# Router logits formed per token tile, an earlier first gather, and paired small matmuls in a transformer block with a mixture of experts

## The chip, the cores and the metric

The kernel is written for Trainium2, and it uses one NeuronCore of the chip. Its engines are TensorE (PE, matrix products), VectorE (DVE), ScalarE (ACT), GpSimd (POOL) and SyncE (SP, which here issues the large DMA transfers). They run side by side and wait for each other through semaphores. The metric is the device time of one execution in microseconds (us), lower is better. The time of the kernel before is the median of three runs.

## What is computed

One layer on 256 tokens of width 1024, all in float32: an attention branch in which each token reads its 64 best-scored tokens, a gated linear-attention branch (GLA) that works in chunks of 64 tokens, and then a mixture of 32 experts of which each token takes 4.

```python
h = _rmsnorm(x, norm1_g) * (1.0 + sc1) + sh1
proj = h @ w_in
...
# GLA, for one chunk of 64 tokens (step); S is the running state
qe = qn * jnp.exp(gn)
A = jnp.einsum('bhid,bhjd->bhij', qe, kn * jnp.exp(-gn))
A = jnp.where(causal, A, 0.0)
o = jnp.einsum('bhij,bhjv->bhiv', A, vn) + jnp.einsum('bhid,bhdv->bhiv', qe, S)
S = S * jnp.exp(g_last).swapaxes(-1, -2) + jnp.einsum('bhjd,bhjv->bhdv', kn * jnp.exp(g_last - gn), vn)
...
x = x + gt1 * (merged @ w_out)
h2 = _rmsnorm(x, norm2_g) * (1.0 + sc2) + sh2
x = x + gt2 * _moe(h2, router_w, router_b, w_gate_up, b_gate_up, w_down, b_down)
...
# _moe
logits = (xt @ router_w + router_b).astype(jnp.float32)
top_v, top_e = lax.top_k(logits, TOP_K)
wts = jax.nn.softmax(top_v, axis=-1)
...                      # each token to its 4 experts, gate and up products, SwiGLU, down product, weighted sum
```

## The kernel before

There are 256 tokens, so two token tiles of 128 (`t` = 0 and 1), and 1024 features, so eight feature tiles (`KT` = 8).

**First part.** TensorE goes through the weight pieces (512 columns each, 2 MB, four slots in turn) in the order written in `PIECES`. Each result goes to one of eight PSUM banks; the list `PLAN` numbers these tiles and says whether ACT ("A") or DVE ("V") takes each out. `begin` waits until the tile that held the bank eight places earlier is taken, and `full` tells the taker. The order of the engines' work is the order of the code: nothing is scheduled.

**Three small parts of GLA** lie in it. `AT` holds the 64x64 score blocks: 16 products, whose results for even chunks go to PSUM partitions 0 to 63 and for odd chunks to 64 to 127. `state_step(n)` makes the update of the state after chunk `n-1`: four products that contract over 64 rows, rows 0 to 63 of the array for odd `n` and 64 to 127 for even `n`. Tiles `o0` to `o3` are the outputs: 16 products with `AT` (64 rows, 64 columns) and 12 with the state (128 rows, 64 columns), written alternately.

**Router part.** After the last output piece (`wo3`), DVE adds the result to the residual (`take_wo`), ACT squares and sums it, `second_norm(t)` forms the inverse root and `h2`. TensorE transposes `h2` (tiles `hh0` to `hh3`; ACT copies them to `h2T`). Tile `rp` holds four partial sums of the logits for all 256 tokens, in four 32-row groups; ACT copies it, and four products with `stack` and the bias make the logits `rl`. DVE takes the four largest per token (`chosen`), TensorE counts with `before` (a strict triangle of ones) how many earlier tokens chose each expert (`rt`: ranks and totals). From this DVE forms `blocks` (blocks of 64 slots per expert), `slot_id` and, with the help of tile `te`, the tables that the expert loop reads (`tables_ready`).

**Expert loop.** It has one pass per block of 64 slots. A pass is made of gate and up products (32 products of 512 columns, in two column halves of the array, from `gu_slot`), the gather of the next block's tokens (`gather`, products of `h2` with the 0/1 matrix `sel`), its transposes into `xg`, and the down products (from `dn_slot`). The weights of expert 0 are loaded as soon as the slots are free of pieces; those of expert `e` >= 1 slot by slot as soon as the pass that used the slot last is done (SP, lines 343 and 348). So the loop's transfers start with the loop. The gather of block 0 stands ahead of the loop:

```python
            e0 = dve.value_load(table_e[0:1, 0:1], min_val=0, max_val=E - 1)
            select(e0)
            select_weights(e0, slice(0, 1))
```

Before its first product TensorE waits for `xg_out` (the gathered tokens), `selw_ready` and `selw_out`; the last is first signalled by DVE's `memset` of `selwT` (line 1001), which stands behind `select_weights` and thirteen tiny memsets.

Of the kernel before, what the change touches and what calls it, by code (L numbers as in the profile page):

```python
# [13 lines left out]
P = 128  # L14
# [21 lines left out]
    + [(f"vb{i}", "A") for i in range(4)] + [("s1a", "V"), ("s1b", "V"), ("va0", "A"), ("va1", "A")]  # L36
# [9 lines left out]
    + [(f"hh{i}", "A") for i in range(4)] + [("rp", "A"), ("rl", "V"), ("rt", "V"), ("te", "V"), ("wt", "A")]  # L46
# [21 lines left out]
def hybrid_block(nc, x, c, w_ada, b_ada, norm1_g, w_in, w_gate_lr, b_gate, gla_norm_g, w_branch_a, w_branch_b, w_out,  # L68
# [28 lines left out]
    with ExitStack() as ctx:  # L97
# [122 lines left out]
        eofw = sb("eofw", 177, [MAXB + 1, 3 * E])  # L220
        steps8 = small("steps8", [P, T // SLOTS])
# [164 lines left out]
        def _(pool):  # L386
# [34 lines left out]
            for i in range(3):  # L421
# [15 lines left out]
        def _(act):  # L437
# [174 lines left out]

            take("rp", (rpart[:], tile("rp")[:, 0:T], ACT.Copy, {}))
            act.wait_ge(rneg_ready, 1)
            for t in range(TT):
                step(A(eexp[:, t, :], lg[:, t, 0:E], ACT.Exp, bias=nr8[:, t:t + 1]), rexp_ready)

            take("wt", (wT[:], tile("wt")[0:E, 0:T], ACT.Copy, {}))


            act.wait_ge(gath_full, 1)
            step(A(gx[:], bank[2][:], ACT.Copy), gx_out)
            act.wait_ge(gxT_full, 1)
            step(A(xg[:].rearrange("p j s -> p (j s)"), bank[3][:], ACT.Copy), xg_out)
# [26 lines left out]
        def _(dve):  # L651
# [105 lines left out]
            def state(n):  # L757
                for half, name in enumerate((f"s{n}a", f"s{n}b")):
                    wait_tile(dve, name)
                    for j in range(2):  # L760
# [11 lines left out]
            state(1)  # L772
            state(2)
# [89 lines left out]
            def take_wo(i):  # L863
# [69 lines left out]
            wait_tile(dve, "rl")  # L933
            chain(V.tensor_copy(lg[:, :, 0:E], tile("rl")[:, 0:TT * E].rearrange("p (t e) -> p t e", e=E)), out_dve)
            for t in range(TT):
                chain(V.max(r8[:, t, :], lg[:, t, 0:E]))
                step(V.tensor_scalar(nr8[:, t:t + 1], r8[:, t, 0:1], -1.0, None, ALU.mult), rneg_ready if t == 1 else None)
# [12 lines left out]
            wait_tile(dve, "rt")  # L950
            counts = tile("rt")[:, TT * E:TT * E + E]
# [43 lines left out]
            select(e0)  # L995
# [56 lines left out]
        def _(pe):  # L1052
# [136 lines left out]
            for n in range(NCH):  # L1189
                r = 64 * (n % 2)  # L1190
                for h in range(GH):
# [8 lines left out]
            def state_step(n):  # L1200

                cn = n - 1
                r, t = 64 * (cn % 2), cn // 2
                for half, name in enumerate((f"s{n}a", f"s{n}b")):
                    ps = begin(name)
                    for j in range(2):
                        h = 2 * half + j
                        ins = M(ps[:, j * DV:(j + 1) * DV], kdt[r:r + 64, t, h * P:(h + 1) * P], vb[r:r + 64, t, h * DV:(h + 1) * DV],
                                start=True, stop=True)
                    full(ins)  # L1210
# [6 lines left out]
            state_step(3)  # L1217
# [56 lines left out]
            for i in range(4):  # L1274
                t, half = divmod(i, 2)
                ps = begin(f"o{i}")
                for n in (2 * t, 2 * t + 1):
                    r = 64 * (n % 2)
                    for j in range(2):
                        h = 2 * half + j  # L1280
# [32 lines left out]
            for i in range(4):  # L1313
                t, half = divmod(i, 2)
                pe.wait_ge(h2_ready, i + 1)
                transposes(f"hh{i}", h2, t, half)

            ps = begin("rp")
            wait_out(pe, "hh3")
# [153 lines left out]
```

## Time and profile before

| what | value |
|---|---|
| median of 3 runs | 1477.98 us (1476.35 to 1479.79) |
| the profiled execution's own time | 1480.57 us |
| its span, first to last instruction | 1478.2 us |
| mean granted TensorE clock | 0.984 |
| busy: PE, DVE, ACT, POOL | 1381.5, 498.0, 250.2, 10.6 us |
| HBM read | 482.00 MB, 327 GB/s over the span |
| passes of the expert loop | 36 |

The profile is of one execution, and times in it count from its first instruction. "Busy" is a sum over the whole span, so it doesn't say which engine sets the end at a given moment; the chain of waits does. The granted clock is a share of TensorE's full clock, and its two levels are 1.0 (2.4 GHz) and 0.5 (1.2 GHz). In the trace each float32 product shows as two MATMUL records, so x8 is four products.

### The profile page before, as it was taken

How to read it: one execution, taken by the hardware profiler on the slowest of the kernel's cores; microseconds unless marked ns; L12 is line 12 of the kernel's file. 1: busy time of each engine (PE TensorE's matmuls, PEld its weight loads, DVE VectorE, ACT ScalarE, POOL GpSimd, SP SyncE). 2: the span in 40 equal slices, each digit the busy share in tenths (PEclk: the TensorE clock that was granted, in tenths of full speed). 3: DMA queues.
4: the chain of work that ended last, by engine and by line, in shares of the span. 5: the costliest groups of instructions: out<-in, count | busy, mean ns of one | idle time of the engine just before them, and what ended most of it. 6: DMA issues, size and time to landing. Idle time of an engine off the chain costs nothing.

```text
span 1478.2 us, 17039 instructions
## 1 busy us (share of the span) xinstructions
PE 1381.5 (93%) x6263; PEld 618.4 (42%) x6264; DVE 498.0 (34%) x1029; ACT 250.2 (17%) x427; POOL 10.6 (1%) x34
## 2 busy tenths in 40 slices
PE   5999999999969999999999999999999999989996
PEld 3888445888533333333333333333333333223321
DVE  2150023555553323323323323323323323323233
ACT  2321014210021111111111111111111111111111
POOL 0000000100000000000000000000000000000000
PEclk8999999999969999999999999999999999999998
DMA  9643433699628449999699999979999999999994
GB/s 352 216 166 115 169 114 114 210 344 348 231 114 341 168 172 387 418 419 416 245 418 416 419 418 418 416 301 419 418 418 418 417 417 419 419 417 417 419 419 198
DMA packets 113087, 483.37 MB, mean 327 GB/s; under 512 B 10102, under 2 KB 10266, under 8 KB 80202
## 3 DMA queue, kind: packets, MB, share of 16 engines
q1 hardware_dynamic: 111666, 477.95, 81.2%
q0 software_dynamic: 1056, 4.06, 0.9%
q10 hardware_dynamic: 344, 1.07, 0.2%
q8 instruction: 14, 0.23, 0.1%
q14 instruction: 7, 0.06, 0.0%
HBM read 482.00 MB, written 1.05 MB: 327 GB/s over the span
## 4 chain that ended last, share of the span: by engine, by line
PE 72%; DMA 11%; SPq 9%; ACT 4%; issue 1%; DVE 1%; DVEq 0%; ACTq 0%
PE bank L1397 23%; PE bank L1091 14%; PE bank L1426 13%; DMA gu_slot<-in_w_gate_up 10%; PE bank L1100 7%; SPq L343 4%; SPq L348 4%; PE bank L1356 4%; PE bank L1372 3%; PE bank L1365 1%; DMA piece<-in_w_ada 1%; ACT gx L633 1%; ACT xg L635 1%; ACT actT L637 1%; PE bank L1404 1%
## 5 line engine op out<-in xcount | busy, mean ns | idle before, releaser
L1397 PE MATMUL bank<-gu_slot,xg 128*64 128x512 f32 x2304 | 517.1, 596 | 17.2 <-DMA gu_slot<-in_w_gate_up 16.5
L1397 PEld LDWEIGHTS bank<-gu_slot,xg 128*64 128x64 f32 x2304 | 158.5, 137 | 364.8 <-issue 307.5
L1426 PE MATMUL bank<-dn_slot,actT 128*64 128x512 f32 x1152 | 255.1, 595 | 24.7 <-ACT actT L637 24.7
L1011 DVE TENSOR_TENSOR rowt<-bank,gt 128x512 f32<-128x512 f32 x144 | 92.7, 686 | 389.7 <-PE bank L1372 388.4
L1091 PE MATMUL bank<-hT,piece 128*128 128x256 f32 x704 | 155.1, 382 | 0.0
L1426 PEld LDWEIGHTS bank<-dn_slot,actT 128*64 128x64 f32 x1152 | 79.3, 137 | 177.4 <-issue 144.2
L1091 PEld LDWEIGHTS bank<-hT,piece 128*128 128x128 f32 x704 | 134.6, 192 | 19.5 <-issue 1.1
L631 ACT ACTIVATE sig<-gcl 128x512 f32<-128x512 f32 x36 | 22.7, 630 | 567.7 <-DVE gcl L1029 567.7
L1029 DVE TENSOR_SCALAR gcl<-bank 128x512 f32<-128x512 f32 x36 | 24.9, 692 | 273.6 <-PE bank L1397 273.6
L1015 DVE TENSOR_TENSOR xs<-xs,rowt 128x512 f32<-128x512 f32 x144 | 93.1, 688 | 2.5
L1100 PE MATMUL bank<-piece,hT 128*128 128x512 f32 x192 | 83.4, 593 | 0.0
L1356 PE MATMUL bank<-h,sel 128*64 128x512 f32 x296 | 71.3, 603 | 3.0 <-DVE sel L983 3.0
L1372 PE MATMUL bank<-ysb,selwT 64*128 64x512 f32 x288 | 71.5, 615 | 0.0
L641 ACT ACTIVATE ysb<-bank 128x512 f32<-128x512 f32 x36 | 21.5, 598 | 248.9 <-PE bank L1426 248.9
L1100 PEld LDWEIGHTS bank<-piece,hT 128*128 128x128 f32 x192 | 36.2, 190 | 44.3 <-issue 44.2
L631 ACT ACT_TABLE_LOAD x36 | 46.2, 1283 | 1.2 <-issue 0.6
L890 DVE SCALAR_TENSOR_TENSOR modq<-piece,csig,modq 128x512 f32<-128x512 f32 x56 | 42.1, 752 | 2.0
L1356 PEld LDWEIGHTS bank<-h,sel 128*64 128x64 f32 x296 | 21.5, 139 | 45.7 <-issue 45.7
L1372 PEld LDWEIGHTS bank<-ysb,selwT 64*128 64x128 f32 x288 | 24.8, 186 | 31.8 <-issue 31.8
L1365 PE MATMUL bank<-ident,gx 128*128 128x128 f32 x148 | 24.3, 286 | 12.5 <-ACT gx L633 11.9
L1100 PE MATMUL bank<-piece,mergedT 128*128 128x512 f32 x64 | 27.9, 594 | 0.7 <-DVE mergedT L860 0.7
L1091 PE MATMUL bank<-ybT,piece 128*128 128x256 f32 x128 | 28.0, 379 | 0.0
(279 smaller groups left out, 787.1 us busy)
## 6 DMA issues: line engine op xcount, KB each, us to landing
gu_slot<-in_w_gate_up SPq DMA_DIRECT2D x256, 1024.0 KB, 17.4
dn_slot<-in_w_down SPq DMA_DIRECT2D x128, 1024.0 KB, 17.6
piece<-in_w_in SPq DMA_DIRECT2D x17, 2048.0 KB, 8.3
piece<-in_w_ada SPq DMA_DIRECT2D x12, 2048.0 KB, 12.9
piece<-in_w_branch_a SPq DMA_DIRECT2D x2, 2048.0 KB, 8.6
piece<-in_w_branch_b SPq DMA_DIRECT2D x2, 2048.0 KB, 8.7
piece<-in_w_out SPq DMA_DIRECT2D x2, 2048.0 KB, 8.5
xs<-in_x ACTq DMA_DIRECT2D x1, 1024.0 KB, 8.9
```

What stands on the lines that cost most here:

```text
L343: sp.dma_start(gu_slot[j][:], w_gate_up[0, e, j * P:(j + 1) * P, :] if isinstance(e, int) else w_gate_up[0, ds(e, 1), j * P:(j + 1) * P, : ...
L348: sp.dma_start(dn_slot[i][:], w_down[0, e, rows, :].rearrange("(i p) n -> p i n", p=P) if isinstance(e, int) else w_down[0, ds(e, 1), rows ...
L631: A(sig[:], gcl[:], ACT.Sigmoid, scale=ALPHA).then_inc(sig_ready, 1)
L890: chain(V.scalar_tensor_tensor(dst[:], w[:, k, :], csig[:, k:k + 1], dst[:], ALU.mult, ALU.add), modq_ready if k == KT - 1 else None)
L1011: ins = V.tensor_tensor(rowt[:, t, :], sum_bank[t][q][:], gt2[:, cols_], ALU.mult)
L1015: ins = V.tensor_tensor(xs[:, t, cols_], xs[:, t, cols_], rowt[:, t, :], ALU.add)
L1091: ins = M(ps[:, f * T:(f + 1) * T], w[:, k, a:a + P], src[:, k, :], start=(k == 0), stop=(k == KT - 1))
L1100: ins = M(ps[:], src[:, k, t * P:(t + 1) * P], w[:, k, :], start=(k == 0), stop=(k == KT - 1))
L1356: ins = M(bank[2][64 * q:64 * q + 64, :], sel[:, t, :], h2[:, t, 512 * q:512 * q + 512], start=(t == 0), stop=(t == TT - 1))
L1372: ins = M(sum_bank[t][q][:], selwT[64 * q:64 * q + 64, t * P:(t + 1) * P], ysb[64 * q:64 * q + 64, :], start=True, stop=True)
L1397: ins = M(bank[u][64 * q:64 * q + 64, :], xg[:, k % 4, 64 * (k // 4):64 * (k // 4) + 64], gu_slot[k][:, cols_], start=(k == 0), stop=(k == ...
L1426: ins = M(bank[5][64 * q:64 * q + 64, :], actT[:, f % 4, 64 * (f // 4):64 * (f // 4) + 64], dn_slot[f // 2][:, f % 2, 512 * q:512 * q + 51 ...
```

## The change

1. `state_step(1)` and `state_step(2)` are issued together, product by product in turn (rows 0 to 63 and rows 64 to 127 of the array), and DVE takes them in that order.
2. The products of `AT` and of `o0` to `o3` are reordered so that two that use different halves of the array stand next to each other.
3. `h2` is multiplied by `sc2g` in `take_wo`, before the inverse root is known; `second_norm` then needs one operation per half in place of two.
4. `rp`, its copy and the products with `stack` are gone. The logits of tile `t` are eight products of `h2T` (128x128, stationary) with the router weights (32 columns), and one with the bias; `rl0` stands between the transposes of `t` = 0 and those of `t` = 1.
5. Block 0 is always expert 0's (`steps8[:, 0]` is -1, so each expert has at least one block, even with no token), so its slots are the ranks themselves: `first_slot` and `sel` are made straight after `rt`, ahead of `blocks` and the tables, and the first gather stands ahead of tile `te`, into `bank[6]`, with its transposes in `bank[7]`, ahead of `wt`.

```diff
-    + [(f"hh{i}", "A") for i in range(4)] + [("rp", "A"), ("rl", "V"), ("rt", "V"), ("te", "V"), ("wt", "A")]
+    + [("hh0", "A"), ("hh1", "A"), ("rl0", "V"), ("hh2", "A"), ("hh3", "A"), ("rl1", "V"), ("rt", "V"), ("te", "V"), ("wt", "A")]
...
+            step.settle()
+            step(nc.gpsimd.memset(steps8[:, 0:1], -1.0))
...
                 chain(V.tensor_tensor(xv, xv, tmp[:], ALU.add), x2_ready)
+                cols_ = slice(512 * cc, 512 * cc + 512)
+                step(V.tensor_tensor(h2[:, t, cols_], xv, sc2g[:, cols_], ALU.mult))
...
-                    chain(V.scalar_tensor_tensor(h2[:, t, cols_], xs[:, t, cols_], rs[:, t:t + 1], sc2g[:, cols_],
-                                                 ALU.mult, ALU.mult))
-                    step(V.tensor_tensor(h2[:, t, cols_], h2[:, t, cols_], sh2[:, cols_], ALU.add), h2_ready)
+                    step(V.scalar_tensor_tensor(h2[:, t, cols_], h2[:, t, cols_], rs[:, t:t + 1], sh2[:, cols_],
+                                                ALU.mult, ALU.add), h2_ready)
...
             wait_tile(dve, "rt")
+            for t in range(TT):
+                step(V.scalar_tensor_tensor(first_slot[:, t:t + 1], tile("rt")[:, t * E:t * E + 1], 1.0, chosen[:, t, 0:1],
+                                            ALU.add, ALU.mult))
+            step.settle()
+            for t in range(TT):
+                ins = V.tensor_scalar(sel[:, t, :], iota[:], 1.0, first_slot[:, t:t + 1], ALU.add, ALU.is_equal)
+            ins.then_inc(sel_ready, 1)
...
-            select(e0)
             select_weights(e0, slice(0, 1))
...
             wait_out(pe, "vb3")
-            state_step(1)
+            for half in range(2):
+                begin(f"s1{'ab'[half]}")
+                begin(f"s2{'ab'[half]}")
+                for lower, upper in zip(state_half(1, half), state_half(2, half)):
+                    pass
+                full(lower)
+                full(upper)
             by_token("va", 0, hT)
-            state_step(2)
             by_token("va", 1, hT)
...
-                for n in (2 * t, 2 * t + 1):
-                    r = 64 * (n % 2)
-                    for j in range(2):
-                        h = 2 * half + j
-                        o_ = ps[r:r + 64, j * DV:(j + 1) * DV]
+                for j in range(2):
+                    h = 2 * half + j
+                    vcols = slice(h * DV, (h + 1) * DV)
+                    for n in (2 * t, 2 * t + 1):
+                        r = 64 * (n % 2)
                         a = (h * 2 + n // 2) * CHUNK
-                        ins = M(o_, AT[r:r + 64, a:a + CHUNK], vb[r:r + 64, t, h * DV:(h + 1) * DV], start=True, stop=(n == 0))
+                        ins = M(ps[r:r + 64, j * DV:(j + 1) * DV], AT[r:r + 64, a:a + CHUNK], vb[r:r + 64, t, vcols],
+                                start=True, stop=(n == 0))
+                    for n in (2 * t, 2 * t + 1):
+                        r = 64 * (n % 2)
                         if n > 0:
-                            ins = M(o_, qe[:, h, n * CHUNK:(n + 1) * CHUNK], S[n][:, h * DV:(h + 1) * DV], start=False, stop=True)
+                            ins = M(ps[r:r + 64, j * DV:(j + 1) * DV], qe[:, h, n * CHUNK:(n + 1) * CHUNK], S[n][:, vcols],
+                                    start=False, stop=True)
...
-            for r in range(2):
-                for q in range(4):
-                    k = 4 * r + q
-                    ins = M(ps[32 * q:32 * q + 32, 0:T], wr[:, k, :], h2T[:, k, :], start=(r == 0), stop=(r == 1))
...
+            for t in range(TT):
+                for half in range(2):
+                    pe.wait_ge(h2_ready, 2 * t + half + 1)
+                    transposes(f"hh{2 * t + half}", h2, t, half)
+                ps = begin(f"rl{t}")
+                for k in range(KT):
+                    if k % 4 == 0:
+                        wait_out(pe, f"hh{2 * t + k // 4}")
+                    M(ps[:, 0:E], h2T[:, k, t * P:(t + 1) * P], wr[:, k, :], start=(k == 0), stop=False)
+                full(M(ps[:, 0:E], ones[0:1, :], rb[:], start=False, stop=True))
...
+            pe.wait_ge(sel_ready, 1)
+            gather(bank[6])
+            ps = begin("te")
+            pe.wait_ge(eofc_ready, 1)
+            full(M(ps[0:3 * E, 0:MAXB + 1], eofw[:], ident[0:MAXB + 1, 0:MAXB + 1], start=True, stop=True))
+            pe.wait_ge(gx_out, 1)
+            gather_transposes(bank[7])
+            ps = begin("wt")
```

How the instructions stand on TensorE, at three places. The numbers with L are lines of each kernel's own file, and a name like `S_74` is the buffer `S2`.

First place: the outputs of GLA on TensorE (`AT` score blocks, `vb` values, `S_73` to `S_75` the states after chunks 0, 1 and 2). Of before, from the start of `o0`:

```order
L1283 MATMUL bank<-vb,AT 64x256 x3
L1285 MATMUL bank<-S_73,qe 64x256
L1283 MATMUL bank<-vb,AT 64x256
L1285 MATMUL bank<-S_73,qe 64x256
L1283 MATMUL bank<-vb,AT 64x256 x3
L1285 MATMUL bank<-S_73,qe 64x256
```

Of the kernel changed, the end of `o1` (token tile 0) and the start of `o2` (token tile 1):

```order
L1299 MATMUL bank<-vb,AT 64x256 x2
L1304 MATMUL bank<-S_73,qe 64x256
L1299 MATMUL bank<-vb,AT 64x256 x2
L1304 MATMUL bank<-S_74,qe 64x256
L1304 MATMUL bank<-S_75,qe 64x256
L1299 MATMUL bank<-vb,AT 64x256 x2
```

Before, each `AT` product but a few has a state product behind it; now two `AT` products stand together, and in token tile 1 two state products too.

Second place: the logits on TensorE, behind the last output piece (`h_85` is `h2`, `rpart` the copy of `rp`, `rb` the bias). Before:

```order
L1107 MATMUL bank<-ident,h_85 128x128 x16
L1324 MATMUL bank<-h2T,wr 32x256 x8
L1329 MATMUL bank<-stack,rpart 128x32
L1330 MATMUL bank<-rb,ones 128x32
L1329 MATMUL bank<-stack,rpart 128x32
L1330 MATMUL bank<-rb,ones 128x32
```

Changed:

```order
L1116 MATMUL bank<-ident,h_85 128x128 x8
L1342 MATMUL bank<-wr,h2T 128x32 x8
L1343 MATMUL bank<-rb,ones 128x32
L1116 MATMUL bank<-ident,h_85 128x128 x8
L1342 MATMUL bank<-wr,h2T 128x32 x8
L1343 MATMUL bank<-rb,ones 128x32
```

The logits of token tile 0 now stand ahead of the transposes of token tile 1.

Third place: on TensorE from the end of `rt` (last product of the counts) to the expert loop (`eofw` is the input of `te`, `wts` that of `wt`, `sel` and `gx` those of the gather and of its transposes). Before:

```order
L1339 MATMUL bank<-chosen,ones 128x32
L1342 MATMUL bank<-ident,eofw 96x49
L1348 MATMUL bank<-ident,wts 32x128 x2
L1378 TENSOR_LOAD table_n
L1378 ISA x2
L1356 MATMUL bank<-h_85,sel 64x512 x4
L1365 MATMUL bank<-ident,gx 128x128 x4
```

Changed:

```order
L1352 MATMUL bank<-chosen,ones 128x32
L1358 MATMUL bank<-h_85,sel 64x512 x4
L1374 MATMUL bank<-ident,eofw 96x49
L1367 MATMUL bank<-ident,gx 128x128 x4
L1382 MATMUL bank<-ident,wts 32x128 x2
L1396 TENSOR_LOAD table_n
L1396 ISA x2
```

The gather moved from behind the load of `table_n` to the place right behind `rt`, ahead of `te`, and its transposes ahead of `wt`.

## Rows read from the trace of the kernel before

**Rows 1.** The page: span, granted clock in 40 slices, one group (busy, mean ns).

```profile
span 1478.2 us, 17039 instructions
...
PEclk8999999999969999999999999999999999999998
...
L1029 DVE TENSOR_SCALAR gcl<-bank 128x512 f32<-128x512 f32 x36 | 24.9, 692 | 273.6 <-PE bank L1397 273.6
```

**Rows 2.** Chain that ended last, late in the expert loop (start, us, what).

```profile
930.34 24.93 DMA gu_slot<-in_w_gate_up
```

**Rows 3.** Chain that ended last, 120 to 300 us.

```profile
130.83 1.47 PE bank L1193 x32
...
190.39 1.92 PE bank L1208 x8
...
245.47 1.00 PE bank L1283 x6
246.48 0.58 PE bank L1285 x2
...
260.12 3.77 PE bank L1252 x32
```

**Rows 4.** Line 1170's own instructions: min/median/max ns, first to last start.

```profile
L1170 PE MATMUL bank<-kiT,qiT x32: 272/374/378, 71.6 to 74.1; 64*128 64x128 f32 x16, 64*128 64x256 f32 x16
```

**Rows 5.** Timeline, 405 to 445 us (start, duration, engine, line; idle before).

```profile
411.30 1.04 PE L1107 MATMUL bank<-ident,h 128*128 128x128 f32 x8
...
414.38 1.28 ACT L609 ACT_TABLE_LOAD   x1
...
415.43 0.75 DVE L877 SCALAR_TENSOR_TENSOR h<-xs,rs,sc2g 128x512 f32<-128x512 f32 x1
...
415.78 1.07 ACT L452 ACTIVATE h2T<-bank 128x512 f32<-128x512 f32 x2
...
418.35 1.12 PE L1107 MATMUL bank<-ident,h 128*128 128x128 f32 x4 [0.27 <-DVE h L879]
...
420.20 1.93 PE L1324 MATMUL bank<-h2T,wr 128*32 128x256 f32 x16 [0.73 <-issue]
...
424.38 0.63 PE L1330 MATMUL bank<-rb,ones 1*128 1x32 f32 x2
...
427.19 0.61 PE L1335 MATMUL bank<-chosen,before 128*128 128x32 f32 x2 [2.17 <-DVE chosen L940]
...
428.89 0.61 PE L1339 MATMUL bank<-chosen,ones 128*128 128x32 f32 x2
429.60 0.29 DVE L953 TENSOR_TENSOR over<-bank,steps 128x128 f32<-128x128 f32 x1 [0.96 <-PE bank L1339]
...
431.33 0.52 PE L1342 MATMUL bank<-ident,eofw 49*96 49x49 f32 x2 [1.83 <-DVE eofw L960]
...
432.64 0.27 DVE L970 TENSOR_SCALAR of_block<-bank,expert_no 96x49 f32<-96x49 f32 x1
...
433.62 0.13 DVE L977 CAST table_n<-cum 1x1 int32<-1x1 f32 x1
434.81 0.42 DVE L983 TENSOR_SCALAR sel<-iota,slot_id 128x64 f32<-128x64 f32 x2 [1.05 <-issue]
...
435.37 3.35 PE L1356 MATMUL bank<-h,sel 128*64 128x512 f32 x8 [2.98 <-DVE sel L983]
...
436.16 0.27 DVE L1001 MEMSET selwT<- 128x256 f32 x1
...
440.75 1.94 PE L1397 MATMUL bank<-gu_slot,xg 128*64 128x512 f32 x8 [0.69 <-ACT xg L624]
```

**Rows 6.** Stretches: us, busy by engine, granted clock, DMA share, GB/s.

```profile
414.00:416.00 2.00, 0.00 (x0) 0.00 (x0) 1.49 (x7) 1.81 (x4) 0.00 (x0) 0.59 1.04 438
...
424.00:426.00 2.00, 1.01 (x4) 0.81 (x4) 0.83 (x6) 0.00 (x0) 0.00 (x0) 0.50 0.00 0
438.00:439.00 1.00, 0.72 (x4) 0.00 (x0) 0.20 (x1) 0.24 (x1) 0.00 (x0) 0.87 0.00 0
```

More of the change, by code:

```diff
@@ L220, in hybrid_block @@
         eofw = sb("eofw", 177, [MAXB + 1, 3 * E])
+        first_slot = small("first_slot", [P, TT])
         steps8 = small("steps8", [P, T // SLOTS])
@@ L611, in _ @@
                 take_T(h2T, "hh", i)
-            take("rp", (rpart[:], tile("rp")[:, 0:T], ACT.Copy, {}))
-            act.wait_ge(rneg_ready, 1)
             for t in range(TT):
+                act.wait_ge(rneg_ready, t + 1)
                 step(A(eexp[:, t, :], lg[:, t, 0:E], ACT.Exp, bias=nr8[:, t:t + 1]), rexp_ready)
+            act.wait_ge(gath_full, 1)
+            step(A(gx[:], bank[6][:], ACT.Copy), gx_out)
+            act.wait_ge(gxT_full, 1)
+            step(A(xg[:].rearrange("p j s -> p (j s)"), bank[7][:], ACT.Copy), xg_out)
             take("wt", (wT[:], tile("wt")[0:E, 0:T], ACT.Copy, {}))
[L621 to L624, printed above, removed]
             act.wait_ge(tables_ready, 1)
@@ L754, in _, with state @@
                                      ke[:, 2 * i:2 * i + 2, :], ALU.mult), out_dve)
-            def state(n):
-                for half, name in enumerate((f"s{n}a", f"s{n}b")):
+            def state(*numbers):
+                for half, n in itertools.product(range(2), numbers):
+                    name = f"s{n}{'ab'[half]}"
                     wait_tile(dve, name)
+                    if n > 1:
+                        step.settle()
                     for j in range(2):
@@ L770, in state @@
                 step.settle()
[L772 to L773 removed]
+            state(1, 2)
             state(3)
@@ L1188, in _ @@
             wait_out(pe, "kb1")
-            for n in range(NCH):
-                r = 64 * (n % 2)
-                for h in range(GH):
+            for m, h in itertools.product(range(NCH // 2), range(GH)):
+                for n in (2 * m, 2 * m + 1):
+                    r = 64 * (n % 2)
                     a = (h * 2 + n // 2) * CHUNK
@@ L1312, in _ @@
             by_token("wo", 1, mergedT)
[L1313 to L1319, printed above, removed]
-            pe.wait_ge(late_in, 48)
-            for r in range(2):
-                for q in range(4):
-                    k = 4 * r + q
-                    ins = M(ps[32 * q:32 * q + 32, 0:T], wr[:, k, :], h2T[:, k, :], start=(r == 0), stop=(r == 1))
-            full(ins)
-            ps = begin("rl")
-            wait_out(pe, "rp")
-            for t in range(TT):
-                M(ps[:, t * E:(t + 1) * E], rpart[:, t * P:(t + 1) * P], stack[:], start=True, stop=False)
-                ins = M(ps[:, t * E:(t + 1) * E], ones[0:1, :], rb[:], start=False, stop=True)
-            full(ins)
+            pe.wait_ge(late_in, 48)
+            for t in range(TT):
+                for half in range(2):
+                    pe.wait_ge(h2_ready, 2 * t + half + 1)
[6 more added lines that the diff above has]
+                full(M(ps[:, 0:E], ones[0:1, :], rb[:], start=False, stop=True))
             ps = begin("rt")
-            pe.wait_ge(chosen_ready, TT)
+            pe.wait_ge(chosen_ready, 1)
             M(ps[:, 0:E], before[:], chosen[:, 0, :], start=True, stop=True)
+            pe.wait_ge(chosen_ready, 2)
             M(ps[:, E:2 * E], ones[:], chosen[:, 0, :], start=True, stop=False)
@@ L1339, in _, with gather, gather_transposes @@
             full(M(ps[:, 2 * E:3 * E], ones[:], chosen[:, 1, :], start=False, stop=True))
+            def gather(into, also=None):
+                for t in range(TT):
+                    for q in range(2):
+                        ins = M(into[64 * q:64 * q + 64, :], sel[:, t, :], h2[:, t, 512 * q:512 * q + 512],
+                                start=(t == 0), stop=(t == TT - 1))
+                        if also is not None and t == 0 and q == 0:
+                            ins.then_inc(also, 1)
+                ins.then_inc(gath_full, 1)
+            def gather_transposes(into):
+                for j in range(4):
+                    ins = nc.tensor.transpose(into[:, j * P:(j + 1) * P], gx[:, j * P:(j + 1) * P], ident[:])
+                ins.then_inc(gxT_full, 1)
+            pe.wait_ge(sel_ready, 1)
+            gather(bank[6])
             ps = begin("te")
@@ L1349, in _ @@
             full(ins)
-            def gather(also=None):
-                for t in range(TT):
-                    for q in range(2):
-                        ins = M(bank[2][64 * q:64 * q + 64, :], sel[:, t, :], h2[:, t, 512 * q:512 * q + 512],
-                                start=(t == 0), stop=(t == TT - 1))
-                        if also is not None and t == 0 and q == 0:
-                            ins.then_inc(also, 1)
-                ins.then_inc(gath_full, 1)
-            def gather_transposes():
-                for j in range(4):
-                    ins = nc.tensor.transpose(bank[3][:, j * P:(j + 1) * P], gx[:, j * P:(j + 1) * P], ident[:])
-                ins.then_inc(gxT_full, 1)
             def scatter():
@@ L1408, in _ @@
                 pe.wait_ge(sel_ready, g2_)
-                gather(gu_used[KT - 1])
+                gather(bank[2], gu_used[KT - 1])
                 pe.wait_ge(ucl_ready, g1_)
```

37 lines of the change are left out of this document (18 added, 19 removed), and 2 rows, old and new, of the table PLAN.

## The prediction

> **What bounds the kernel now.** I read the page's granted clock first, then the chain of waits, then the timeline of the stretch ahead of the expert loop. The clock row [rows 1] shows full clock except in slice 12 and at the ends. In the first part the chain of waits is TensorE's own work almost without a gap: the small GLA products stand in it one behind another [rows 3]. So time taken off TensorE there moves all that follows, as long as the weight pieces and the other engines keep up. From the last output piece (411.5 us) to the first product of the loop (440.75) the chain changes hands between DVE, ACT and TensorE, and each small step counts [rows 5].
>
> In the loop it is TensorE first and the weight stream later (a 24.93 us stretch of weight transfers in the chain at 930) [rows 2]. Both start with pass 0: expert 1's first slot is only loaded when pass 0 has used it. So whichever of the two sets the end, it moves by as much as the start of pass 0 moves. Expert 0's own weights are no obstacle: the transfers are over before 424 to 426 us, where they move 0 GB/s [rows 6].
>
> **States 1 and 2 together.** A state step, four products of 256 columns over 64 rows, takes 1.92 us [rows 3]. That two row halves can work at once is seen at line 1170: eight products of 128 and eight of 256 columns, alternating rows, take from 71.6 to about 74.4 (last start 74.1 plus 0.3), 2.8 us [rows 4]. By the price below of 0.44 for 256 columns and half of it for 128, one after the other would take 5.3. So the second step hides under the first: -1.9 us (bounds -1.9 and 0). DVE takes the states in the other order, but TensorE reads them only at 246.48 [rows 3].
>
> **AT.** Its 16 products take 1.47 us [rows 3], four with one column half, then four with the other. Perfect pairing gives half, -0.7; nothing gives 0. I take -0.5.
>
> **The GLA outputs.** At 245.47 three AT products take 1.00 us; then a state product takes 0.58, and the AT product behind it about as much [rows 3]. Let a slot of 256 columns cost a, a change of form (64x64 to 128x64 or back) c. The 0.58 is a + c. The state step, four slots and one change, gives 4a + c = 1.92. So a = 0.45, c = 0.13. Three AT products and the change behind them would be 3a + c = 1.48 in a row; they took 1.00, which is 2a + c: the second and third, or the first and third, share a slot. The whole stage, 245.47 to 260.12, is 14.65 us: 28 products less two shared slots, and 24 changes, 26a + 24c = 14.8. After the change each of four tiles has per head one AT pair, a change, one state product or pair, a change: 16 slots and 16 changes, 16 x 0.58 = 9.2. That is -5.4 us. Bounds: no pair shares a slot, -0.5 (8 fewer changes, two shared slots lost: 28a + 16c = 14.7, near 0); no change costs anything, 16a = 7.2, -7.4.
>
> What hides next: DVE and ACT take the four outputs sooner and wait for the same bias rows as before; what they make of them is read only behind the next two weight pieces, and TensorE waits for none of it now.
>
> Here the skill has a rule against the change. The shared slot at 245.47 is of two products that write halves of the same PSUM bank, `o0` [rows 3]. The Trainium skill, TensorEngine Tiling (Array Packing), section "Restrictions and Gotchas", says that different row tiles cannot access the same PSUM bank at the same time. By that rule the eight AT pairs would be sixteen slots, 3.6 us more; by the row they are eight. I go with the row, and keep the other as a rival below.
>
> **The router part, in the clock of the rows** (the shift of the parts ahead comes on top).
>
> - DVE: `second_norm(1)` now has one operation of 0.75 per half from 415.43 on [rows 5], where it had two; `h2` of tile 1 is complete at 416.9 in place of 418.3. The operations added in `take_wo` (0.7 each) run while ACT squares.
> - But that isn't what TensorE waits for next. The logits of tile 0 need ACT's copy of `hh0`, and ACT reaches it only at 415.78, behind a table load of 1.28 at 414.38 [rows 5]; two copies take 1.07. So `rl0` starts at 416.3.
> - Its price: a product of 32 columns with a 128x128 stationary takes 0.43 (five from 427.19 to 429.50, the first 0.6; rows 5), the bias product 0.6. Nine: 0.2 + 8 x 0.43 + 0.6 = 4.2, to 420.5. Its order ahead of the transposes of tile 1 delays these: they could have started at 416.3.
> - Eight transposes, 1.12 for four [rows 5]: 2.2, to 422.7. ACT's copy of `hh3` ends at 423.4, under the first half of `rl1`. Nine products again, 4.2: `rl1` is full at 426.9. Before, eight narrow products from 420.20, a copy and four products ended at 425.0 [rows 5]. So the logits come 1.9 later.
> - DVE: tile 0's four largest are done under that. From the end of the logits to `rt` it was 2.2 for two tiles (427.19 less 425.0); for one it is about 1.2: 428.1. One of the five `rt` products is done ahead: 1.9, to 430.0 (before 429.5).
> - DVE adds `first_slot` and the first `sel` ahead of `blocks`: two tiny operations of some 0.15 and the 0.42 of `sel` [rows 5], with waits 0.75. `blocks` starts at 430.85, where it was 429.60.
> - `te` is now behind the gather. The gather starts at 430.9 and takes 3.35 at the half clock [rows 5], to 434.25; `te` (0.5) ends at 434.8. DVE needs it 3.04 after `blocks` (432.64 less 429.60), at 433.9. So 0.9 more. `tables_ready` followed 1.1 later (433.75): now 435.9, 2.15 later.
> - Behind the tables: `selwT`'s memset ended at 436.43, 2.68 after them. Without `select`, about 0.35 less: 2.33, so 438.25. The gather's copy, transposes and second copy (0.6, 1.1, 0.6 and gaps) end about 436.8, sooner. TensorE's loads of `table_n` and `table_w` fit in the 2.3. Pass 0 starts at 438.3 against 440.75: **-2.4 us**. Bounds: `te` not late and short gather, -4.5; products at 0.6 in place of 0.43, -0.
>
> **The clock.** TensorE fell to 1.2 GHz at about 414.4, some 2 us after its last transposes, stayed there through `rp`, `rl` and `rt`, and rose to 2.4 GHz at about 438.3, in the gather of 512-column products; pass 0 began 2 us later at full clock [rows 5, 6]. After the change the gather ends 4 us ahead of pass 0, with only `te`, four transposes and `wt` between. I expect pass 0 to start at 1.2 GHz. Price: four products of that form take 3.35 at the low clock, 1.94 at the high (435.37 and 440.75; rows 5), so 3.35 us at the low clock lose 1.4. The last rise came 2.9 us after such work began. I take +1.5 (bounds 0 and +2.8, twice the stretch).
>
> **Sum.** -1.9 -0.5 -5.4 -2.4 +1.5 = -8.7. The profiled execution took 1480.57, so 1471.9 for it; it stands 2.6 above the median of the runs, 1477.98. I forecast the median: 1469.3.
>
> **Rivals.**
>
> - *Forecast*, pass 0 starts cold: 1469.3, own range 1467.5 to 1471.5. Chance 0.47.
> - *Pass 0 starts warm*, since the gather lifts the clock and the small work behind it holds it: 1467.8. For it, the same gather did lift it; against, the 2 us that sufficed for the fall at 414.4. Chance 0.22.
> - *The clock rises in the router part*, as TensorE is now busy from 416.3 to 426.9 without a stop. Then `rl1`, the transposes, `rt` and the gather take half: the gather alone -1.4, `rl1` and `rt` -2.5, some of it lost to the wait for `te`: about -4, with no cold start 1464. Against: `rp` and `rt` were dense too and lifted nothing. Chance 0.10.
> - *Row tiles exclude each other on one bank*: 3.6 less gained, 1472.9. Against it is the 1.00 us. Chance 0.12.
> - *Nothing shares a slot and the router part gains nothing* (products of 0.6): about 1477 to 1479. Line 1170 speaks against it. Chance 0.05, with 0.04 for "no change".
> - *Slower*: `steps8` gives every expert a block. If an expert had no token, the loop would have 37 passes in place of 36 [rows 1], and a pass takes about 28.8 us ((1478.2 - 440.75) / 36): 1498. It decides with the first empty expert. The reference's own choices, counted for these inputs, have none: the fewest are 2 tokens, and four experts exceed 64, which makes the 36. Chance 0.01. The rest, 0.03, is for something unseen in the loop, either way.
>
> **Numbers.** About 0.2%, 3 us, is what a measurement here can tell from no change. The first four cases are all faster than 1475, 0.91, and part of the rest: faster 0.93, same 0.05, slower 0.02. The range from 1464 to 1473.5 takes in the first four cases.
>
> **What the new profile would show.** Line 1216 once with x16 in about 1.9 us; the GLA outputs in about 9.2; `rl0` starting right after ACT's first `hh` copy; `te` behind the gather, DVE idle ahead of `of_block`; pass 0 about 26.8 us after the last output piece (29.3 before); 36 passes. A clock below 1 at the start of pass 0 decides between the first two cases. Wrong would be: outputs of 12 to 13 us (the bank rule), logits that end well after 15.4 us behind the last piece, or weights of expert 0 that are waited for.

## The result, and the profile after

The changed kernel takes 1467.11 us (median of 5 runs, 1466.88 to 1471.06). The kernel before takes 1476.54 (1474.74 to 1479.79, 5 runs, three of them those that the forecast started from). The ratio is 0.9938, 95% interval 0.9925 to 0.9950: faster by 0.6%, 2.2 us under the forecast. The profiled execution took 1467.80 us.

The page of the changed kernel, answering [rows 1]: span, granted clock, and one group.

```profile
span 1466.0 us, 17062 instructions
...
PEclk9999999999969999999999999999999999999998
...
L1038 DVE TENSOR_SCALAR gcl<-bank 128x512 f32<-128x512 f32 x36 | 24.9, 691 | 272.6 <-PE bank L1411 272.6
```

There are 36 passes as before. The first slice of the clock was 8 and is 9, and that is no work of the change: between 28 and 40 us the granted clock was 0.57 in the traced execution of before and 1.00 in this one, ahead of anything that was touched. `AT` starts at 127.45 in place of 130.83. These 3.4 us have to be taken off the 12.2 by which the spans differ.

The chain that ended last, answering [rows 3]:

```profile
127.45 1.08 PE bank L1202 x32
...
170.69 2.00 PE bank L1216 x16
...
200.35 1.92 PE bank L1216 x8
...
239.59 0.58 PE bank L1299 x4
240.17 0.57 PE bank L1304 x2
...
244.79 0.58 PE bank L1304 x4
...
248.85 3.77 PE bank L1268 x32
```

`AT` takes 1.08 us (1.47 before). Two state steps take 2.00 together (before 1.99 and 1.92, apart), and the third, alone, still 1.92. In the outputs x4 (two products, one from each half of the array) costs the same 0.58 as x2. The stage goes from 239.59 to 248.85: 9.26 us, in place of 14.65. It now has 16 slots and 16 stretches of one form, where it had 26 and 24. From the start of `AT` to the end of the last output piece it is 272.8 us (127.45 to 400.21), where it was 280.6 (130.83 to 411.47): 7.9 us less.

The timeline from the last output piece to the loop, answering [rows 5] (start, duration, engine, line; idle before):

```profile
398.75 1.45 PE L1109 MATMUL bank<-piece,mergedT 128*128 128x512 f32 x3
...
403.05 1.28 ACT L613 ACT_TABLE_LOAD   x1
...
405.18 3.47 PE L1342 MATMUL bank<-wr,h2T 128*128 128x32 f32 x16 [4.10 <-ACT h2T L456]
...
414.56 0.63 PE L1343 MATMUL bank<-rb,ones 1*128 1x32 f32 x2
...
417.73 0.61 PE L1352 MATMUL bank<-chosen,ones 128*128 128x32 f32 x2
419.18 3.50 PE L1358 MATMUL bank<-h,sel 128*64 128x512 f32 x8 [0.84 <-DVE sel L959]
...
423.09 0.27 DVE L980 TENSOR_SCALAR of_block<-bank,expert_no 96x49 f32<-96x49 f32 x1 [1.04 <-PE bank L1374]
...
426.73 3.68 PE L1411 MATMUL bank<-gu_slot,xg 128*64 128x512 f32 x8 [2.47 <-DVE selwT L1010]
...
433.80 2.79 PE L1411 MATMUL bank<-gu_slot,xg 128*64 128x512 f32 x11
```

The logits of tile 0 wait for ACT's copies behind the table load, those of tile 1 are complete 15.0 us behind the last piece (13.5 before), DVE waits 1.04 us for `te`, and pass 0 starts 26.5 us behind the piece (29.3 before), but takes 3.68 us for its first four products in place of 1.94. The stretches of the same kernel, answering [rows 6]:

```profile
422.00:424.00 2.00, 1.59 (x12) 0.82 (x8) 0.89 (x8) 0.60 (x1) 0.00 (x0) 0.91 0.00 0
424.00:426.00 2.00, 0.26 (x3) 0.00 (x0) 1.03 (x13) 1.35 (x3) 0.00 (x0) 0.95 0.00 0
426.00:428.00 2.00, 1.27 (x4) 0.59 (x6) 1.17 (x11) 0.79 (x1) 0.00 (x0) 0.50 0.05 12
...
432.00:434.00 2.00, 2.00 (x10) 0.73 (x8) 0.08 (x1) 0.00 (x0) 0.00 (x0) 0.85 0.78 324
```

The clock rises near the end of the gather, and has fallen again when pass 0 starts. The next slot's products start 7.1 us after pass 0 (4.2 before, 440.75 to 444.97), and the next pass is 2.9 us late too, counted from pass 0 (30.54 in place of 27.69; first the kernel before, then the changed one):

```profile
468.44 1.89 PE L1397 MATMUL bank<-gu_slot,xg 128*64 128x512 f32 x8
```

```profile
457.27 1.89 PE L1411 MATMUL bank<-gu_slot,xg 128*64 128x512 f32 x8
```

So the whole loss is made in pass 0. It stays at 2.8 to 2.9 us up to pass 18; behind that the changed kernel makes up 1.0 us, a drift like that among the four traces that start warm, whose loops differ by 0.8. At the end of the span 1.8 are left: from the start of pass 0 it is 1039.3 us, before 1037.5.

So the spans add up: -3.4 (start, not the change) -7.9 (pairs) -2.8 (pass 0 nearer to the piece) +1.8 (cold start of the loop) = -12.3, measured 12.2.

### The profile page after: what moved, and what is told of

Its sections match the earlier page's. It is cut to its first block, busy times and chain, and to the rows that moved or that the text cites. A ratio compares the mean times of both kernels' runs of the same rounds, so it can differ in the third digit from the quotient of the medians.

```text
span 1466.0 us, 17062 instructions
## 1 busy us (share of the span) xinstructions
PE 1378.1 (94%) x6275; PEld 619.7 (42%) x6276; DVE 498.9 (34%) x1032; ACT 249.7 (17%) x426; POOL 10.7 (1%) x35
## 4 chain that ended last, share of the span: by engine, by line
PE 73%; DMA 12%; SPq 9%; ACT 4%; issue 1%; DVE 1%; DVEq 0%; ACTq 0%
PE bank L1411 24%; PE bank L1100 14%; PE bank L1440 13%; DMA gu_slot<-in_w_gate_up 10%; PE bank L1109 8%; SPq L345 4%; SPq L350 4%; PE bank L1358 4%; PE bank L1390 3%; PE bank L1367 1%; ACT gx L633 1%; ACT xg L635 1%; ACT actT L637 1%; DMA piece<-in_w_ada 1%; DMA piece<-in_w_in 1%
## 5 line engine op out<-in xcount | busy, mean ns | idle before, releaser
L1367 PE MATMUL bank<-ident,gx 128*128 128x128 f32 x148 | 24.3, 287 | 12.3 <-ACT gx L633 11.9
```

## The experiments

Ratios are to the kernel before on the same chip, medians of 5 runs or more; "behind the piece" is from the end of the last output piece to pass 0's first product, and "loop" from there to the end of the span.

**pairs_only** is the kernel before with parts 1 and 2 alone; **router_only** is it with parts 3, 4 and 5 alone; **no_early_gather** is the changed kernel without part 5:

```diff
-            pe.wait_ge(sel_ready, 1)
-            gather(bank[6])
             ps = begin("te")
...
             wait_out(pe, "te")
+            pe.wait_ge(sel_ready, 1)
+            gather(bank[2])
```

> Only the paired products (states, AT, GLA outputs), router part as before. If the shared slots are the gain: the outputs take 9.3 us in place of 14.65, the states 2.0 for two, AT 1.1, and the time is 7.7 us below the kernel before (ratio about 0.9948). If the time saved on TensorE were given back to a weight piece or to DVE's sums behind it, the later pieces would show idle time ahead of them and the ratio would be nearer 0.998.

> Only the router part of the change (logits per tile, early multiplication, first gather ahead of the tables), GLA as before. Theory: pass 0 starts 26.5 us behind the last output piece (29.3 before) and gives all of it back by starting at 1.2 GHz (2.9 us): ratio 0.998 to 1.001. Rival: the router part is the larger half of what the change gains (ratio 0.997 or less), which holds if pass 0 starts at full clock in most executions.

> The changed kernel with its first gather put back behind the tables, as before. Theory: logits per tile and early multiplication are neutral on the path (rt ends 18.1 us behind the last output piece in both), so pass 0 starts 29.3 us behind it, but at full clock: the time equals that of the changed kernel within 1 us (ratio 0.993 to 0.995). Rival: the first gather is a true gain and the clock's fall has another cause: then this one is 2.5 to 3 us slower than the changed kernel (ratio 0.996) and its pass 0 is cold as well.

pairs_only: 1467.82 us, ratio 0.9947 (0.9935 to 0.9960). router_only: 1475.63, ratio 0.9994 (0.9985 to 1.0003), no difference that can be told. no_early_gather: 1468.17, ratio 0.9951 (0.9939 to 0.9963). The start of pass 0 in pairs_only, in router_only, and in no_early_gather with the gather ahead of it:

```profile
428.50 1.94 PE L1411 MATMUL bank<-gu_slot,xg 128*64 128x512 f32 x8 [0.69 <-ACT xg L625]
```

```profile
433.95 3.68 PE L1398 MATMUL bank<-gu_slot,xg 128*64 128x512 f32 x8 [1.99 <-DVE selwT L1008]
```

```profile
423.31 3.64 PE L1350 MATMUL bank<-h,sel 128*64 128x512 f32 x8 [2.99 <-DVE sel L984]
...
428.98 1.94 PE L1403 MATMUL bank<-gu_slot,xg 128*64 128x512 f32 x8 [0.69 <-ACT xg L622]
```

The last pieces end at 398.88, 406.94 and 399.16, so pass 0 stands 29.6, 27.0 and 29.8 us behind. What follows: the time comes from the pairs. Parts 3 and 4 alone bring nothing (29.8 against 29.6). The early gather brings 3.3 us (29.8 to 26.5), and takes the warm start away. no_early_gather came out just above the 0.993 to 0.995 expected: by the traces the early gather is worth 3.3 less a cold start of 1.8 to 2.9, so 0.4 to 1.5 us, which these intervals can't tell from nothing.

**filler** asks whether the clock is what is lost: three useless products of 512 columns ahead of the loop in the changed kernel.

```diff
+            for _ in range(3):
+                M(bank[6][:], ident[:], h2[:, 0, 0:512], start=True, stop=True)
```

> The changed kernel with three 512-column products of no use on TensorE between wt and pass 0 (they write a bank that is free then). If pass 0 is cold because TensorE does little in the 2.5 us ahead of it, it now starts at full clock, its first products take 1.9 in place of 3.7 us, and the time is 2 to 3 us below the changed kernel (ratio about 0.992). If the clock falls all the same, the time is that of the changed kernel.

1466.84 us, ratio 0.9933 (0.9920 to 0.9946). Its filler, pass 0, and the clock:

```profile
423.88 4.09 PE L1385 MATMUL bank<-h,ident 128*128 128x512 f32 x6
427.90 1.94 PE L1412 MATMUL bank<-gu_slot,xg 128*64 128x512 f32 x8
```

```profile
424.00:426.00 2.00, 2.00 (x4) 0.90 (x4) 1.39 (x18) 1.22 (x3) 0.00 (x0) 0.50 0.04 12
426.00:428.00 2.00, 2.00 (x6) 0.56 (x6) 0.99 (x4) 0.61 (x1) 0.00 (x0) 0.85 0.00 0
```

Pass 0 starts warm, but 28.8 us behind the piece: the filler itself ended later than `selwT`, at 427.97 against 425.83. The loop is 1036.9 us, and the 2 to 3 us expected in the time did not come. Over the traces of all kernels here the loop is 1036.7 to 1037.5 us in the four that start it warm (before, pairs_only, no_early_gather, filler), and 1039.2 to 1040.4 in nine of the ten that start it cold, the tenth, narrow_per_tile, with 1037.7. On average that is 2.5 us for a cold start. What pass 0 alone loses is read closer: the next slot starts 4.2 us after pass 0 in all four warm traces and 5.7 to 7.1 in the ten cold ones, 1.4 to 2.9 more, the more the later the clock rises. Heating with a filler costs as much as it gives.

**copy_first** moves ACT's table load behind the first tile's copies; **grouped_o** orders the outputs pair, state, state, pair, so that neighbours of one form join:

```diff
-            step(A(warm[:, 1:2], ident[:, 0:1], ACT.Exp))
-            for i in range(4):
-                take_T(h2T, "hh", i)
+            take_T(h2T, "hh", 0)
+            take_T(h2T, "hh", 1)
+            step(A(warm[:, 1:2], ident[:, 0:1], ACT.Exp))
+            take_T(h2T, "hh", 2)
+            take_T(h2T, "hh", 3)
```

```diff
+                for ins in itertools.chain(scores(0), states(0), states(1), scores(1)):
+                    pass
```

> The changed kernel, with ACT's copies of hh0 and hh1 ahead of the table load and its tiny exponential. The prediction said that rl0 waits for that load (1.4 us from the root to the first copy). If so, rl0 starts about 3.5 us behind the last output piece in place of 5.0 and pass 0 1.4 us sooner; then the gain is 1.4 us (ratio 0.9930). Rival: the logits of tile 0 are hidden anyway, and nothing moves.

> The changed kernel, with the GLA outputs in the order AT pair, state, state, AT pair, so that the form changes half as often (8 times in place of 16); the number of shared slots is the same. If a change costs 0.13 to 0.15 us, the stage takes 8.1 us in place of 9.3. Rival: the 0.15 is not of the change of form but of reading or starting each short product; then it stays at 9.3.

copy_first: 1465.65 us, ratio 0.9922 (0.9908 to 0.9936). grouped_o: 1466.25, ratio 0.9921 (0.9908 to 0.9934). The logits of tile 0 in copy_first, then the chain of grouped_o:

```profile
402.39 3.48 PE L1344 MATMUL bank<-wr,h2T 128*128 128x32 f32 x16 [2.58 <-ACT h2T L456]
```

```profile
239.66 0.58 PE bank L1298 x4
240.24 1.01 PE bank L1306 x4
241.25 1.01 PE bank L1298 x8
...
247.90 3.77 PE bank L1268 x32
```

TensorE waits 2.58 us for the copies in place of 4.10, and pass 0 comes 25.0 us behind the piece (26.5): the table load was on the path. In grouped_o two slots cost 1.01 and one 0.58, so a slot is 0.43 and a change of form 0.15. The chain has 9 stretches in place of 16, so 7 changes fewer (the expectation counted 8); the stage takes 8.24 us, 1.0 less than 9.26. By these prices the change's own 5.4 us in the outputs are ten slots, 4.3, and eight changes, 1.2.

**filler_front** puts four useless products of 512 columns ahead of `rl0`, where TensorE stands idle, so that it meets the logits warm:

```diff
                 ps = begin(f"rl{t}")
+                for _ in range(4 if t == 0 else 0):
+                    M(ps[:], ident[:], h2[:, 0, 0:512], start=True, stop=True)
```

> The changed kernel, with four 512-column products of no use between the transposes of token tile 0 and rl0, where TensorE waits 4.1 us for ACT. If it is this idle stretch that takes the clock to 1.2 GHz for the whole router part, the clock now holds through rl0 and the transposes (16 records of rl0 in 1.8 in place of 3.5 us), and pass 0 starts 3 us or more sooner. Rival: the 32-column products themselves let the clock fall; then it falls some us later, in rl0 or rl1, and the gain is under 2 us.

1465.75 us, ratio 0.9921 (0.9905 to 0.9936).

```profile
405.13 1.97 PE L1344 MATMUL bank<-wr,h2T 128*128 128x32 f32 x16 [0.57 <-ACT h2T L456]
...
408.80 3.59 PE L1344 MATMUL bank<-wr,h2T 128*128 128x32 f32 x16 [0.34 <-ACT h2T L456]
```

```profile
406.00:408.00 2.00, 2.00 (x18) 1.92 (x18) 0.46 (x3) 0.00 (x0) 0.00 (x0) 1.00 1.04 438
408.00:410.00 2.00, 1.66 (x11) 1.45 (x8) 0.53 (x5) 1.29 (x3) 0.00 (x0) 0.58 0.98 414
```

`rl0` takes 1.97 us at the full clock, 3.47 at half. Then the clock falls although TensorE was busy nearly throughout since 400.1: in the first of these stretches PE is busy 2.00 of 2 us. The filler's gain ends with `rl0` and the transposes: pass 0 is 24.8 us behind the piece, 1.7 sooner, which is the rival's "under 2 us". That it is the 32-column products that let the clock fall is not shown.

**narrow_pooled** undoes the direct logits alone (as before: both tiles transposed, then narrow partial products of 256 columns, one copy, `stack`); **narrow_per_tile** has the narrow form for each token tile apart, with the second tile's transposes between. Every kernel with a narrow form (these two, best and best_te_mid) also has one more wait of TensorE ahead of the loop, for the copy of `wt`:

```diff
+            tile_transposes(0)
+            partial_logits(0)
+            tile_transposes(1)
+            logits_of(0)
+            partial_logits(1)
+            logits_of(1)
...
             wait_out(pe, "te")
+            wait_out(pe, "wt")
```

> The changed kernel, with the logits of each token tile formed as in the kernel before (four partial sums of 32 rows, a copy, one product with stack), but tile by tile. Theory: the direct form is the dearer one (3.5 us for eight products with a 128x128 stationary, against about 1.0 for the narrow ones and 1.6 for copy, sum and bias), so rl1 is full 2.5 us sooner and pass 0 starts 2 to 2.5 us sooner. Rival: the copy by ACT and the waits between engines cost as much, and it moves by less than 0.5 us.

> The changed kernel with the direct logits alone undone: both token tiles are transposed, then eight narrow products of 256 columns, one copy, and per tile a stacking product and the bias; the norm with one operation per half, the early gather and the pairs stay. If the direct form is what cost the time that the shorter norm gives, the logits are complete about 12.5 us behind the last output piece (13.5 in the kernel before, less 1.0 for the norm; 15.0 in the changed kernel), and pass 0 starts 24.0 us behind it in place of 26.5: ratio near 0.992 against 0.9938, which 5 rounds can barely tell, so the reading is the trace. Rival: the delay is the place of rl0 ahead of the second tile's transposes or the table load, not the form; then the logits come 15 us behind the piece again. With partial logits per tile it was 22.2 us; what lies between that and this run is what splitting by tile gives.

narrow_per_tile: 1463.93 us, ratio 0.9916 (0.9901 to 0.9931). narrow_pooled: 1464.77, ratio 0.9912 (0.9896 to 0.9927). The timelines of TensorE, first narrow_per_tile:

```profile
405.25 1.08 PE L1347 MATMUL bank<-h2T,wr 128*32 128x128 f32 x16 [4.10 <-ACT h2T L456]
...
408.75 0.65 PE L1347 MATMUL bank<-h2T,wr 128*32 128x128 f32 x16
...
410.19 0.40 PE L1354 MATMUL bank<-rb,ones 1*128 1x32 f32 x2
```

```profile
407.71 1.93 PE L1343 MATMUL bank<-h2T,wr 128*32 128x256 f32 x16 [0.78 <-ACT h2T L456]
...
411.90 0.63 PE L1349 MATMUL bank<-rb,ones 1*128 1x32 f32 x2
```

Eight products for 128 tokens take 1.08 us in the narrow form, in four row groups of the result, and 3.47 in the direct one, both begun as the clock falls (0.74 and 0.83 from 404 to 406 us, 0.50 from 406 to 408). The pieces end at 400.28 and 400.26, so the logits are complete 10.3 us behind the piece per tile, 12.3 pooled and 15.0 direct; pass 0 follows at 22.2, 24.2 and 26.5. The direct form costs 2.7 us against the pooled one in the logits and 2.3 at pass 0. But the pooled kernel also has both tiles' transposes first, and narrow_per_tile had the clock on its side for its second tile:

```profile
408.00:410.00 2.00, 1.51 (x24) 1.17 (x22) 0.99 (x7) 1.09 (x4) 0.00 (x0) 0.91 1.05 442
```

It was 0.91 there and 0.94 from 410 to 412 us, where narrow_pooled and the changed kernel had 0.50. So the 2.0 us between 24.2 and 22.2 are not all owed to the split by tile. The form by itself is best read from copy_first against best (below), which keep the tiles in the same order and both stay at 0.50 from 404 us to the gather.

**te_mid** moves only `te` in the changed kernel, between the gather's two token tiles; **best** puts grouped_o, copy_first and narrow_per_tile together; **best_te_mid** is best with te_mid's move:

```diff
+                if t == 0:
+                    ps = begin("te")
+                    pe.wait_ge(eofc_ready, 1)
+                    full(M(ps[0:3 * E, 0:MAXB + 1], eofw[:], ident[0:MAXB + 1, 0:MAXB + 1], start=True, stop=True))
```

> The changed kernel with only the te product moved, between the gather's first and second token tile. In the changed kernel te ran 422.62 to 423.0 behind a gather of 3.50 us (419.18), and VectorE waited 1.04 us for it ahead of of_block. If that wait is what the early gather costs the tables, of_block starts about 1.0 us sooner, pass 0 about 0.9 us sooner (25.6 us behind the last output piece in place of 26.5), ratio near 0.993 against 0.9938. Rival: the wait moves to xg (gather's end, copy on ScalarE, transposes) and pass 0 stands where it was.

> The three edits that each moved pass 0 or the outputs forward, together: outputs in the order pair, state, state, pair (8 changes of form fewer), the first token tile's two copies ahead of ScalarE's table load, and partial logits of each token tile in the narrow form with a copy and a stacking product. Compared with the changed kernel's trace (first product of pass 0 at 426.73) the edits alone had it 1.0, 2.8 and 4.3 us sooner, the second of which holds 1.3 us of an earlier last output piece that is no work of the edit, so 1.5 counts. If the three lie one after another on the chain: 6.8 us sooner, pass 0 near 420, a ratio near 0.989. Rival: copies first and narrow form share the same hidden stretch (the table load lies behind the first partial logits in the narrow form, and rows of the second tile are waited for), so that together they give little more than the narrow form alone: pass 0 near 421.5, ratio near 0.991.

> The kernel 'best' with the te product put between the gather's first and second token tile (half of the gather, 1.8 us at the low clock, comes behind te). If te's place behind the gather makes the routing tables late by what VectorE stood idle ahead of of_block (1.04 us in the changed kernel's trace), pass 0 starts about 0.9 us sooner than in 'best' and the ratio falls by 0.0006, which is under what 5 rounds can tell, so the reading is in the trace: VectorE's idle time ahead of of_block near 0, and selwT's end nearer to the gather's end. Rival: TensorE then ends the gather later and pass 0 waits for ScalarE's xg in place of selwT, so that nothing is gained.

te_mid: 1467.94 us, ratio 0.9943 (0.9924 to 0.9961). best: 1461.02, ratio 0.9892 (0.9874 to 0.9909). best_te_mid: 1462.03, ratio 0.9901 (0.9884 to 0.9918). The end of the logits in copy_first; DVE, ACT and TensorE in te_mid; TensorE in best; ACT and TensorE in best_te_mid:

```profile
411.77 0.63 PE L1345 MATMUL bank<-rb,ones 1*128 1x32 f32 x2
```

```profile
422.22 0.27 DVE L980 TENSOR_SCALAR of_block<-bank,expert_no 96x49 f32<-96x49 f32 x1
...
425.33 0.27 DVE L1010 MEMSET selwT<- 128x256 f32 x1
425.54 0.60 ACT L623 ACTIVATE xg<-bank 128x512 f32<-128x512 f32 x1 [1.21 <-PE bank L1367]
```

```profile
401.39 0.82 PE L1353 MATMUL bank<-h2T,wr 128*32 128x128 f32 x16 [2.58 <-ACT h2T L456]
402.64 1.69 PE L1120 MATMUL bank<-ident,h 128*128 128x128 f32 x8 [0.42 <-DVE h L885]
...
405.09 1.08 PE L1353 MATMUL bank<-h2T,wr 128*32 128x128 f32 x16
...
407.19 0.63 PE L1360 MATMUL bank<-rb,ones 1*128 1x32 f32 x2
...
419.72 3.68 PE L1436 MATMUL bank<-gu_slot,xg 128*64 128x512 f32 x8 [1.99 <-DVE selwT L1014]
```

```profile
419.14 0.36 ACT L456 ACTIVATE wT<-bank 32x256 f32<-32x256 f32 x1
...
420.82 3.46 PE L1441 MATMUL bank<-gu_slot,xg 128*64 128x512 f32 x8 [1.78 <-issue]
```

In te_mid DVE no longer waits ahead of `of_block`, and `selwT` is done 0.9 us sooner. But `xg` now ends at 426.14, and pass 0 starts at 426.82, 26.6 us behind the piece (26.5 in the changed kernel): the rival held, pass 0 waits for `xg`. The two traces aren't at equal clock, though: in te_mid it was 0.50 through gather and transposes, in the changed kernel it rose before the transposes. Beside router_only, whose gather was at 0.50 throughout (27.0), te_mid is 0.4 us sooner. In best pass 0 stands at 419.72, 7.0 us sooner than in the changed kernel. 1.2 of it is there before the outputs start (238.36 against 239.59), 1.0 comes from the outputs, and 4.7 from the router part (21.8 us behind the piece). So copy_first and narrow_per_tile seem not to add up: 1.5 and 4.3 alone, 4.7 together. Most of what is missing is the clock. In best the second tile's partial products start 7.2 us behind the piece (405.09 less 397.94), in narrow_per_tile 8.5, so the copies' gain is there but for 0.2 us (on the way TensorE now waits 0.42 for DVE's `h2` of the second tile, L885). But from there to the end of the logits it is 2.7 us in best, at 0.50, and 1.8 in narrow_per_tile, at 0.91 to 0.94: 0.9 us that the edits don't explain. Against copy_first, at nearly the same clock, the narrow form has the logits complete at 9.9 us behind the piece in place of 13.5, and pass 0 at 21.8 in place of 25.0: the direct form costs 3.6 and 3.2 us.

In best_te_mid pass 0 is 22.3 us behind the piece, no gain there either, but this run doesn't test the place of `te` alone. `xg` is ready at 419.25, TensorE's added wait for the copy of `wt` ends with it at 419.50, and only then does it load the loop's first table entry; pass 0 comes 1.3 us later. In te_mid, without that wait, the load runs under `xg`'s copy, and pass 0 follows `xg` by 0.7. best beats the kernel before by 1.1%; its interval does not overlap that of the changed kernel.

## Why the prediction was right

- **Pairs**: forecast -1.9 -0.5 -5.4 = -7.8. Measured in the trace: -1.9 (one 2.00 where 1.99 and 1.92 stood), -0.4 and -5.4, so -7.7; the whole stretch from `AT` to the last piece is 7.9 shorter. The other 0.2 is in the two weight pieces behind state steps 1 and 2, which take 27.66 us in one piece and took 13.93 each. pairs_only alone is 0.9947 of before, 7.8 us, while the router part alone is 0.9994.
- **The bank rule** would have made 3.6 us more of the outputs. The eight x4 rows of `AT` products at 0.58, the price of one product and one change, show that two products that write halves of one PSUM bank from two halves of the array go side by side. The Trainium skill, TensorEngine Tiling (Array Packing), "Restrictions and Gotchas", says otherwise; by this trace the measurement decides.
- **Router part**: forecast pass 0 at 26.8 us behind the piece, measured 26.5. The steps held one by one: `rl0` behind the table load, logits at 15.0 (15.4), `rt` done at 18.1 (18.5), `te` late by 1.04 (0.9), the wait ended by `selwT`.
- **The clock**: pass 0 starts cold, as the likeliest case had it. The term was mis-sized: I put +1.5, from the four products in view. The products behind them are slow too, until the clock rises in the stretch from 432 to 434 us: 2.9 us at the next slot, just past the upper bound of 2.8; 1.8 are left at the end of this trace, some 2.5 over all traces.
- **The sum**: -8.7 forecast, -9.4 between the medians; -7.9 -2.8 +1.8 = -8.9 in the traces. The router part, forecast at -0.9 with its clock, is -1.0: here two errors of 0.3 and 0.4 us, in the clock and in the start of pass 0, cancel, and that is luck. That pass 0 started warm (1467.8 forecast) isn't what happened, although its time is nearer than 1469.3: 1.4 of the 2.2 us between forecast and result are the base, as before's median was 1477.98 in the three runs that the forecast started from and 1476.54 in the five. The start of the loop, not the median, tells the two cases apart.

What the prediction didn't ask is whether part 4 pays. It priced the logits 1.9 us later than before and took that as given; with the narrow form kept, pass 0 would stand 2.3 us (pooled) to 3.2 us (per tile, best beside copy_first) sooner.

## What to carry to other kernels

Small products that use different halves of the array (here 64 rows, 256 columns, float32) cost one slot for two when they stand next to each other, even where they write the two halves of one PSUM bank; count slots and changes of form, each with its own price, from two rows. A form that saves a copy and a summing step is not shorter for that: ask for the columns that are moved and for the stationary matrix that is loaded (eight products of 32 columns behind a full 128x128 load took three times as long as eight narrow ones of 128 columns). And when a dense piece of work is moved away from the start of a long loop, look at what clock the loop then starts at. Before two kernels' stretches are compared, compare their granted clocks: most of what seemed lost between two edits here was a clock that one trace had and the other had not.

## What the runs showed of the hardware

- The same gather of 3.4 to 3.7 us ends with a rise of the granted clock in some traces (before, pairs_only, no_early_gather, the changed kernel) and not in others: in router_only and filler, for two, the clock is 0.50 all the way through and behind it. What decides it I haven't settled.
- In filler_front the clock falls from 1.00 to 0.50 behind two microseconds (406 to 408) in which TensorE was busy all the time with 32-column products and transposes. In the changed kernel, with such products from 405.18 to 408.65 and from 411.04 to 415.19, it stays at 0.50 from 406 to 416 us.
- A product of 32 columns with a 128x128 stationary takes 0.22 us at the full clock and 0.43 at the half (from start to start; eight take 1.97 and 3.48 us, `rl0` in filler_front and in copy_first).
